# A gated linear mixer whose running states keep the blocks between heads, and softmax weights made between two halves of the bias

## The reference

```python
# softmax attention, per block of 128 queries; 4 heads, 2 maps m per head
s = jnp.einsum('bqhmd,bkhmd->bhmqk', qb, kb) * scale + bias        # causal
p = jax.nn.softmax(s, axis=-1)
w = p[:, :, 0] - lam * p[:, :, 1]
out = jnp.einsum('bhqk,bkhd->bqhd', w, vb)

# gated linear attention: 4 heads, keys of 32, values of 64, 8 chunks of 64 tokens
attn = jnp.einsum('nbhqd,nbhkd->nbhqk', q_dec, k_inv) * causal
o_intra = jnp.einsum('nbhqk,nbhkv->nbhqv', attn, vc)
def step(state, inp):
    q_c, k_c, v_c, dec_c = inp
    o_inter = jnp.einsum('bhqd,bhdv->bhqv', q_c, state)            # per head
    state = state * dec_c[..., None] + jnp.einsum('bhkd,bhkv->bhdv', k_c, v_c)
    return state, o_inter
_, o_inter = lax.scan(step, state0, (q_dec, k_end, vc, chunk_decay))
o = o_intra + o_inter
```

## Time and profile before

| what | value |
|---|---|
| time, median of 3 runs | 2685.53 us (2676.68 to 2692.46) |
| the profiled execution's own time | 2676.34 us |
| its span | 2674.6 us |
| PE busy | 2476.3 us, 93% of the span |
| DVE busy | 1125.2 us, 42% |
| ACT busy | 408.7 us, 15% |
| POOL busy | 234.6 us, 9% |
| mean granted clock of TensorE | 0.973 |

### The profile page before, as it was taken

One profiled execution on the slowest core, in us unless ns is written; L12 is line 12 of the kernel. 1 busy time (PEld: TensorE's weight loads), 2 busy tenths in 40 slices (PEclk: granted clock), 3 DMA queues, 4 the chain that ended last, 5 costly groups with the idle time before them and its releaser, 6 DMA issues. The chain is left out here.

```text
span 2674.6 us, 53350 instructions
## 1 busy us (share of the span) xinstructions
PE 2476.3 (93%) x23953; PEld 1821.3 (68%) x23953; DVE 1125.2 (42%) x2073; ACT 408.7 (15%) x955; POOL 234.6 (9%) x215
## 2 busy tenths in 40 slices
PE   7999989799999997999899799888889979999999
PEld 3587655578787774588777565444458747888888
DVE  4652654511111116336765433233354465435542
ACT  2122540300000002000231200000010441110000
POOL 0000000122222210001101100000010301000000
PEclk9999999899999999999999799999999989999999
DMA  8351326699999994114455899999942201222311
GB/s 323 129 183 60 123 79 243 261 361 409 406 407 408 407 407 171 48 48 146 130 163 220 324 422 422 422 423 423 422 189 94 72 1 64 81 93 79 119 72 47
DMA packets 89851, 594.92 MB, mean 222 GB/s; under 512 B 10880, under 2 KB 34368, under 8 KB 44392
## 3 DMA queue, kind: packets, MB, share of 16 engines
q1 hardware_dynamic: 74888, 558.54, 52.7%
q0 software_dynamic: 12000, 22.48, 3.4%
q10 hardware_dynamic: 2736, 10.49, 1.0%
HBM read 574.33 MB, written 16.10 MB: 221 GB/s over the span
## 5 line engine op out<-in xcount | busy, mean ns | idle before, releaser
L1287 PE MATMUL moe_ps<-room,moe_xs 128*32 128x256 f32 x9616 | 554.9, 383 | 54.9 <-DMA room<-in_experts 40.1
L1287 PEld LDWEIGHTS moe_ps<-room,moe_xs 128*32 128x32 f32 x9616 | 388.9, 111 | 219.0 <-issue 63.4
L1287 PE MATMUL moe_ps<-room,moe_hid_t 128*32 128x256 f32 x4640 | 261.8, 379 | 9.8 <-DMA room<-in_experts 6.9
L1287 PEld LDWEIGHTS moe_ps<-room,moe_hid_t 128*32 128x32 f32 x4640 | 183.3, 110 | 87.7 <-issue 11.7
L1620 DVE TENSOR_TENSOR moe_hid<-moe_silu,moe_ps 128x512 f32<-128x512 f32 x32 | 22.0, 687 | 316.4 <-PE moe_ps L1287 273.4
L1549 DVE SCALAR_TENSOR_TENSOR x_feat<-moe_ps,mod,x_feat 128x512 f32<-128x512 f32 (+1 forms) x144 | 95.9, 730 | 125.9 <-PE moe_ps L1349 115.5
L1492 ACT ACTIVATE moe_silu<-moe_ps 128x512 f32<-128x512 f32 x32 | 19.1, 597 | 758.5 <-PE moe_ps L1287 724.6
L1640 DVE TENSOR_SCALAR moe_y<-moe_ps,moe_gates 128x256 f32<-128x256 f32 x42 | 17.7, 478 | 254.7 <-PE moe_ps L1287 254.7
L1330 POOL DMA_INDIRECT acc<-moe_y,moe_sum_ids x42 | 69.0, 1644 | 332.3 <-DVE moe_y L1640 323.8
L2079 PE MATMUL mlstm_psg<-h_feat,room 128*128 128x384 f32 x256 | 90.4, 497 | 1.3 <-ACT room L2175 1.3
L1850 PE MATMUL v_ps<-room,h_feat 128*128 128x256 f32 x384 | 86.0, 382 | 0.0
(11 more groups left out here) (724 smaller groups left out, 3831.1 us busy)
## 6 DMA issues: line engine op xcount, KB each, us to landing
room<-in_experts SPq DMA_DIRECT2D x144, 2048.0 KB, 36.7
room<-in_experts SPq DMA_DIRECT2D x67, 1024.0 KB, 12.6
moe_slot<-in_experts SPq DMA_DIRECT2D x22, 1024.0 KB
feed_f_slots<-in_ffn_gate SPq DMA_DIRECT2D x11, 1024.0 KB, 4.9
feed_f_slots<-in_ffn_up SPq DMA_DIRECT2D x11, 1024.0 KB, 4.8
feed_f_slots<-in_ffn_down SPq DMA_DIRECT2D x8, 1408.0 KB, 6.3
room<-in_ada_w SPq DMA_DIRECT2D x10, 1024.0 KB, 5.0
qk_ada_w<-in_ada_w SPq DMA_DIRECT2D x8, 1024.0 KB, 4.8
```

Of the source, the lines that this page charges most:

```text
L1287: mm = pe.matmul(group_ps(part, g)[32 * q:32 * q + 32], turned[:, k * GROUP:(k + 1) * GROUP], weights[:, m, q], start=(k == 0 and g != 1), ...
```

## The change

Three things are changed, all in the second block's mixers.

1. **States without the mask.** `grow(n)` is one instruction: decayed state plus the outer product read straight from PSUM. The table `heads`, its load, its 1 KB per partition and the semaphore `states` are gone. The states now hold the blocks between heads, so `linear_mix` reads a head's own block alone: matmuls of 32 keys by 64 value columns, two per head and block of 128 tokens, where there were two for a pair of heads. The semaphore `grown` counts states now, where it counted masked products.
2. **The last outer product is left out**: `outer(7)` on PE and `grow(7)` on DVE. `pool_product(0)` still waits for seven states, `pool_product(1)` for six.
3. **Order on DVE**: `weights(u - 1)` stands between the bias of the first map and the bias of the second, where it stood behind both.

The core of the diff:

```diff
-                    pe.wait_ge(sig["grown"], N - 1 + t)
+                    pe.wait_ge(sig["grown"], N - 1 - t)
@@ linear_mix(pair)
-                    pe.wait_ge(sig["states"], 1)
+                    pe.wait_ge(sig["grown"], N - 1)
                     for t in range(LT):
-                        for n in (2 * t, 2 * t + 1):
-                            pe.matmul(to[:, n * C:(n + 1) * C], state(n)[:, pair * P:(pair + 1) * P],
-                                      q_dec[:, n * C:(n + 1) * C], start=(n % 2 == 0), stop=False, skip_group_check=True)
                         for h in (2 * pair, 2 * pair + 1):
-                            rows = slice(GLA_DV * (h % 2), GLA_DV * (h % 2 + 1))
+                            rows, keys = slice(GLA_DV * (h % 2), GLA_DV * (h % 2 + 1)), slice(GLA_DK * h, GLA_DK * (h + 1))
+                            for n in (2 * t, 2 * t + 1):
+                                pe.matmul(to[rows, n * C:(n + 1) * C], state(n)[keys, h * GLA_DV:(h + 1) * GLA_DV],
+                                          q_dec[keys, n * C:(n + 1) * C], start=(n % 2 == 0), stop=False, skip_group_check=True)
                             mm = pe.matmul(to[rows, t * P:(t + 1) * P], v[...], att[:, h, t * P:(t + 1) * P], ...)
@@ PE, unit 10
-                        outer(7)
@@ grow(n)
-                    dve.tensor_tensor(grown[:, n % 2], ps[:, (n + 1) % 2, 0:W], T["heads"][:], ALU.mult).then_inc(sig["grown"], 1)
-                    if n + 1 < N:
-                        dve.wait_ge(sig["grown"], n + 1)
-                        step(dve.scalar_tensor_tensor(state(n + 1), state(n), decay[:, n:n + 1], grown[:, n % 2],
-                                                      ALU.mult, ALU.add))
+                    if n:
+                        dve.wait_ge(sig["grown"], n)
+                    dve.scalar_tensor_tensor(state(n + 1), state(n), decay[:, n:n + 1], ps[:, (n + 1) % 2, 0:W],
+                                             ALU.mult, ALU.add).then_inc(sig["grown"], 1)
@@ DVE, unit u
                     for m in range(2):
+                        if m and u >= 1:
+                            weights(u - 1)
                         dve.wait_ge(sig["scores"], 2 * u + m + 1)
                         dve.scalar_tensor_tensor(s[...], ps[...], rq[...], bias[...], ALU.mult, ALU.add)
-                    if u >= 1:
-                        weights(u - 1)
@@ DVE, unit 10
-                        grow(7)
-                        dve.sem_inc(sig["states"], 1)
```

More of the change, by code:

```diff
@@ L2854, in hybrid_tables @@
     T = {"w_lr": sb("w_lr", [P, KT, 32]), "gla_gate_w": sb("gate_w", [P, P]), "keep": sb("keep", [P, LAT]),
-         "causal": sb("causal", [P, P]), "heads": sb("heads", [P, GLA_HEADS * GLA_DV]), "reverse": sb("reverse", [P, P]),
+         "causal": sb("causal", [P, P]), "reverse": sb("reverse", [P, P]),
          "spread": sb("spread", [P, 4, 32]), "back": sb("back", [P, 3, P]), "rel_bias": sb("rel", [32, DA_HEADS])}
@@ L2862, in load @@
     def load(pool, sig):
-        for n in ("w_lr", "bucket", "rel_bias", "never", "gla_gate_w", "spread", "back", "reverse", "keep", "causal", "heads"):
+        for n in ("w_lr", "bucket", "rel_bias", "never", "gla_gate_w", "spread", "back", "reverse", "keep", "causal"):
             dst = T[n] if n in ("bucket", "never") else T[n][:]
@@ L2871, in load @@
                            ).then_inc(sig["pool_w"], 16)
-    T["load"], T["count"] = load, 11 * 16
+    T["load"], T["count"] = load, 10 * 16
     return T
@@ L2901, in hybrid_mixers @@
         q_dec, k_inv, k_end = ya, yc, yd
-        k_tok, grown = z[:].rearrange("p (t c) -> p t c", c=P), low[:].rearrange("p (r w) -> p r w", w=W)
+        k_tok = z[:].rearrange("p (t c) -> p t c", c=P)
         last_root = z
@@ L3121, in _ @@
                         outer(2 * (u - 7) + 1)
-                    elif u == 10:
-                        outer(7)
                     elif u == 11:
@@ L3575, in constants @@
     out["causal"] = ((p[:, None] <= p[None, :]) & (p[:, None] // 64 == p[None, :] // 64)).astype(f)
-    out["heads"] = (p[:, None] // GLA_DK == np.arange(256)[None, :] // GLA_DV).astype(f)
     r, upper = p % 32, (p >= 64).astype(int)
```

## The result

The changed kernel takes 2691.26 us (median of 12 runs, 2681.24 to 2697.01) against 2680.69 us for the kernel before in its 12: a ratio of 1.0031, 95% interval 1.0017 to 1.0045. A second comparison of the same two kernels in a later set of runs gave 1.0015 (0.9999 to 1.0030). So it is slower, by some 8 us in the first comparison and 4 in the second, both inside what the prediction calls no change. The first interval is clear of the +1.7 us (1.0006) that was forecast; the second holds it, and just reaches no change. The median lies in the range on record.

What follows compares the result with a forecast made beforehand. PE was taken as the bound, DVE counting only where PE waits for it. Terms -0.73 + 0 + 0 + 2.4 + 0.24 - 0.2 = +1.7 us on a median of 2685.53 gave 2687 us, range 2676 to 2697.

Steps and rivals of the forecast that it cites:

- Part 4: `linear_mix` reading states block by block: more matmul records and changes of kind, +2.4 us for both pairs, ends -0.8 and +5.0.
- draining rule: In `linear_mix`, a change of tiling mode drains TensorE: 16 changes a pair instead of 8, at 0.1 us each, +0.8 us.
- third rival: Clock falls to half in `linear_mix` with its small matmuls: +12 us, or +6 for a 13.6 us fall; chance 0.09.
- Part 1: Eight masks gone from DVE in units 7 to 16: `turn(9)` and `linear_mix(0)` begin earlier, -0.73 us, ends 0 and -1.15.
- Part 2: Last outer product and `grow(7)` left out, the load of `heads` gone: hidden ahead of PE's wait for `combine(9)`, 0.
- Part 3: Weights moved between the bias halves on DVE: short waits at units 8 and 12 hidden under PE, 0; ends -0.3 and +0.5.
- Part 5: Clearing semaphores between the mixers' end and "hout": seven ranges for six, +0.24 us.
- Part 6: Clock's edges at the stage's end: `sum_first` begun later against the clock's fall, -0.2 us; "hout" at half clock, 0.
- first rival: Small tiles in `linear_mix` are cheap, `linear_mix` at its low end of -0.8: sum -2.5 us, 2683 us; chance 0.27.

Runs made afterwards that it cites:

- half-changes kernel: Changed kernel with both heads' state matmuls first, then both value products, in each block of 128 tokens: 0.9996 of before, a pair 3.01 us.
- doubled kernel in turn: Changed kernel with state matmuls grouped per pair, heads alternating, and `linear_mix` issued twice: one profile, stage 132.7 us, first pair 4.20 us.
- grouped with heads in turn: Changed kernel with a pair's state matmuls all first, alternating between heads, then the value products: 2670.9 us, 0.9974 of before.

## Why the prediction was right or wrong

The sign of the small sum was right and the time lay in the range, but the loss was several times the one forecast: +1.7 us, against +6.3 for the stage in the first two profiles and +8.3 over three profiles each (130.3 to 138.5). That 2691.26 us lies so near the 2687 on record is partly luck. The 2687 stands on a median of 2685.53 of three runs, and the twelve runs of the kernel before have 2680.69, so the base was 4.8 us too high. The range is 21 us wide, most of it the runs' own spread, and would have held no change as well.

- **Part 4 is the step that failed**, by size. "+1.3 us a pair, +2.6 for both; I take +2.4": it measured 5.86 - 3.73 = +2.13 a pair at full clock, +4.3 for both, inside the ends of -0.8 and +5.0, and outside the 4.6 to 5.4 us that were to show it right. A head took 0.73 us where 0.64 was worked out. The way from its first state record to its first of L3031 is 0.37 us, where I had 0.43; a record of the small kind costs 0.06 us, less than my 0.08. The term that was too small is "one matmul of L3031 and back, 0.21": it measured 0.36. The rows showed two records starting together at 2166.17, two at 2166.33, and 0.21 us from there back to L3027. I took each two for one matmul. In the changed kernel, where a head is alone, the two records of one matmul start 0.16 us apart, and the way back comes behind the second:

```profile
2176.80 0.32 PE L3031 MATMUL hym_ps<-h_feat,hy_v 128*64 128x128 f32 x1
2176.96 0.27 PE L3031 MATMUL hym_ps<-h_feat,hy_v 128*64 128x128 f32 x1
```

  With both heads in the group, in the half-changes kernel as before, two records start each time, and the same 0.16 us serves two matmuls:

```profile
2163.33 0.33 PE L3033 MATMUL hym_ps<-h_feat,hy_v 128*64 128x128 f32 x2
2163.49 0.28 PE L3033 MATMUL hym_ps<-h_feat,hy_v 128*64 128x128 f32 x2
```

  The edit didn't only cut the matmuls smaller and change kind more often, it took neighbours apart that had been running side by side.
- **The draining rule.** The prediction took 0.1 us for each change of kind from the rows, and named the Trainium skill (TensorEngine Tiling (Array Packing), Key Properties) for the rule behind it, that a change of tiling mode drains the engine. The runs agree with a price for each change, of 0.15 us (3.01 against 2.10 us for six more). At that price the eight more changes are some 1.2 us of the 2.13 a pair, an estimate, and not the whole of it.
- **The third rival happened** in two profiles of three, at a chance of 0.09; in the third the clock falls only 0.7 us before the second pair's end. In the two the stretch from the first pair to `turn(11)` is 19.1 and 19.2 us against 13.2 at full clock (two pairs of 5.86 and 1.49 between them): +6.0. That it meets the "+6" written down is partly luck, for the fall lasted 17.1 us and not 13.6, with 14.2 to 14.5 of it in this stretch. The prediction had a fall before it where TensorE had hardly paused, at 2142.7, and gave it too little weight. The rival's reason, small rows as such, isn't enough: in the one profile of the doubled kernel in turn they kept the clock.
- **Part 1** held. "I take -0.73": compared at about the same first low stretch, `linear_mix` begins 0.54 to 0.69 us earlier (95.53 to 94.99 and 94.84; 97.50 to 96.96), and `turn(9)` comes 0.66 us earlier against `turn(4)` in the third profile (25.83 to 25.17). At `turn(6)`, with the weights where they were, it is 75.98 to 75.39, -0.59 against the 0.46 worked out.
- **Part 2**, 0: nothing speaks against it; it was not tried alone.
- **Part 3**, 0: the term at `turn(6)` is +0.34, about 0.1 us a unit, and eats more than half of the mask's gain there. With the weights alone moved, it is still there at the stage's end (130.8 against 130.5), and it lies inside the ends of -0.3 and +0.5.
- **Part 5**, +0.24: +0.13.
- **Part 6**, -0.2 and 0. From `turn(11)` to the stage's end the mean of three profiles is 25.7 us after and 24.4 before, +1.3. The clock's edges fall otherwise there; these are too few profiles to price it.
- The ratio's 0.31% of 2680.7 us is 8.3 us, and the stage's mean difference is +8.3. They meet better than either is known: the interval runs from 4.6 to 12.1 us, the second comparison has 4 us, and a profile's stage moves by several us with the clock. In the first profile alone 9.3 us more came from ahead of the stage; that was the execution, since the other two profiles of the changed kernel don't have it.
- The first rival (small tiles cheap) was wrong for this order and right for another: grouped with heads in turn, a pair is 2.10 us, below the low end on record, which had a pair 0.4 us shorter than 3.73.

## What to carry to other kernels

Before matmuls are split into smaller ones on other rows and columns, look at who their neighbours are and how often the kind changes: the same 48 records took 5.86 us with each head's two kinds one behind the other, 3.01 with both heads' states and then both products, and 2.10 grouped and in turn. A duration read from a group in which two instructions lie side by side isn't the price of one alone. And where an edit makes TensorE's matmuls smaller and its stream sparser, the clock can be part of its price, as in two of three profiles here, so look at more than one execution of each kernel before saying where a few microseconds went.

## What the runs showed of the hardware

- The granted clock fell from 2.4 to 1.2 GHz while TensorE's busy time showed no gap (19.2 us at a mean of 0.63 in the changed kernel's third profile), which a reading by busy time alone doesn't foretell. The Trainium skill (TensorE: Matmul & The Clock Gate, the part on the clock gate) has the clock follow how busy the engine has been; the trace agrees only if that is something other than what the profile's PE row counts.
- Records of float32 matmuls of 32 rows by 64 columns start 0.057 us apart on the same rows and columns and on average 0.034 us apart in turn over two places of the array.
- A change between these matmuls and those of 128 rows by 64 columns costs some 0.15 us: a pair took 2.10 us with one change and 3.01 with seven, with the two heads beside each other in both.
- A group of both heads takes hardly longer than a group of one: 0.75 us a round in the half-changes kernel, 0.73 for one head in the changed one.
- The first half-clock stretch of the same kernel before lasted 13.7 us in one execution and 17.1 in two others, which moved the start of `linear_mix` by 2.0 us (95.5 to 97.5 us).
